# Adding the residual by accumulating stores: an early copy into the output, and four stores from GpSimd that add onto it

## The reference, cut to what matters

```python
    mix = jax.nn.sigmoid(gate_conv) * y_conv + jax.nn.sigmoid(gate_m) * y_m
    x = x + rmsnorm(jnp.einsum('btd,de->bte', mix, w_o), g_post_mix)

    hf = rmsnorm(x, g_pre_ff)
    ff = jnp.einsum('btf,fd->btd', jnp.square(jax.nn.relu(jnp.einsum('btd,df->btf', hf, w_ff1) + b_ff1)), w_ff2) + b_ff2
    x = x + rmsnorm(ff, g_post_ff)
```

## Time and profile before

| | |
|---|---|
| Median of 3 runs | 1226.94 us (1226.82 to 1227.23) |
| The profiled execution's own time | 1226.39 us |
| Its span | 1224.8 us |
| Mean granted TensorE clock | 0.996 of full speed |
| TensorE busy | 1200.2 us, 98% of the span |
| DVE, ACT, POOL busy | 866.0, 544.0, 65.4 us |

### The profile page before, as it was taken

The page is one execution under the profiler, slowest core; times in us unless marked ns, Lnnn a source line. Parts: engine busy times, 40 slices in busy tenths (PEclk is TensorE's granted clock), DMA queues, the critical chain, the costliest instruction groups (busy, mean ns, idle before and its releaser), DMA issues.

```text
span 1224.8 us, 22983 instructions
## 1 busy us (share of the span) xinstructions
PE 1200.2 (98%) x8893; PEld 1128.2 (92%) x8893; DVE 866.0 (71%) x1275; ACT 544.0 (44%) x836; POOL 65.4 (5%) x129
## 2 busy tenths in 40 slices
PE   9999999999999999999999999999999999999995
PEld 9999978989797898879999999999999999999994
DVE  6933788988888898887455434338687587585897
ACT  7533443453454345435543222246655453454543
POOL 4020001101100110110000000000000000000000
PEclk9999999999999999999999999999999999999998
DMA  6354226516432651623223232432433233333332
GB/s 222 104 160 147 70 71 222 199 34 224 170 130 69 222 199 34 239 105 104 87 86 88 85 97 74 158 105 67 145 104 104 87 87 104 87 93 98 86 125 73
DMA packets 44680, 145.95 MB, mean 119 GB/s; under 512 B 4756, under 2 KB 7188, under 8 KB 44232
## 3 DMA queue, kind: packets, MB, share of 16 engines
q1 hardware_dynamic: 33048, 103.74, 26.6%
q0 software_dynamic: 11424, 41.23, 9.6%
q10 hardware_dynamic: 144, 0.09, 0.0%
HBM read 120.54 MB, written 24.49 MB: 118 GB/s over the span
## 4 chain that ended last, share of the span: by engine, by line
PE 94%; DVE 3%; ACT 1%; issue 1%; DVEq 0%; POOL 0%; ACTq 0%; POOLq 0%
PE product L2051 73%; PE side L2051 21%; DVE yacc L2041 0%; PE side L2236 0%; ACT yacc L1294 0%; DVE yacc L1942 0%; ACT hhi L1159 0%; ACT cq L1139 0%; DVE hlo L1878 0%; DVE yacc L2045 0%; ACT whi L765 0%; DVE wlo L1916 0%; DVE wlo L1917 0%; DVE common L1942 0%; DVE wlo L1923 0%
## 5 line engine op out<-in xcount | busy, mean ns | idle before, releaser
L2051 PE MATMUL product<-ahi,whi 128*128 128x272 f32 x1232 | 261.7, 292 | 2.8 <-DVE cq L1860 1.6
L2051 PE MATMUL product<-ahi,wlo 128*128 128x272 f32 x1232 | 256.9, 288 | 0.0
L2051 PE MATMUL product<-alo,whi 128*128 128x272 f32 x1232 | 256.9, 288 | 0.0
L1322 DVE TENSOR_TENSOR wlo<-wraw,whi 128x1024 fp32r<-128x1024 f32 x122 | 148.8, 1224 | 114.5 <-ACT whi L765 102.6
L765 ACT ACTIVATE whi<-wraw 128x1024 fp32r<-128x1024 f32 x122 | 127.9, 1054 | 199.3 <-PE product L2051 121.7
L2051 PEld LDWEIGHTS product<-ahi,whi 128*128 128x128 f32 x1232 | 194.8, 188 | 13.1 <-issue 12.3
L2051 PEld LDWEIGHTS product<-alo,whi 128*128 128x128 f32 x1232 | 194.6, 189 | 0.0
L2051 PEld LDWEIGHTS product<-ahi,wlo 128*128 128x128 f32 x1232 | 193.7, 189 | 0.0
L1535 DVE SCALAR_TENSOR_TENSOR accp<-u,wdw,accp 128x512 f32<-128x512 f32 x240 | 163.7, 745 | 0.7 <-DVE accp L1535 0.7
L2051 PE MATMUL side<-hhi,whi 128*128 128x272 f32 x252 | 73.0, 290 | 3.6 <-DVE yacc L1942 1.4
L2051 PE MATMUL side<-hlo,whi 128*128 128x272 f32 x252 | 72.5, 288 | 0.0
(11 more groups left out here) (348 smaller groups left out, 2464.8 us busy)
## 6 DMA issues: line engine op xcount, KB each, us to landing
wraw<-in_wstream SPq DMA_DIRECT2D x176, 512.0 KB, 3.7
crg<-in_c_in POOLq DMA_DIRECT2D x32, 512.0 KB, 6.7
out_c_s<-crg POOLq DMA_DIRECT2D x32, 512.0 KB, 3.2
hb<-head_rows POOLq DMA_DIRECT2D x4, 580.0 KB, 5.3
x<-in_xT SPq DMA_DIRECT2D x4, 544.0 KB, 6.5
sgm<-in_xT SPq DMA_DIRECT2D x1, 2176.0 KB, 9.3
x_rows<-yc SPq DMA_DIRECT2D x1, 2176.0 KB, 10.1
x1b<-x_rows SPq DMA_DIRECT2D x1, 2176.0 KB, 9.5
```

Source lines behind the costliest of these rows:

```text
L1322: V.tensor_tensor(wlo[:, k % RING, :, :], wraw[:, k % 2, :, :], whi[:, k % RING, :, :].bitcast(f32), ALU.subtract).then_inc(lo_done, 1)
L2051: return pe.matmul(out, lhsT, rhs, start=start, stop=stop, skip_group_check=check)
```

## The change

The residual is copied into the output tensor `yT` itself, by the same early instruction that used to fill the scratch tensor. DVE only multiplies in the tail. GpSimd issues the four final stores, with `accum_op=ALU.add`: such a store adds its bytes to what lies at the destination. It waits for the early copy (`x1_moved`) and for each multiplication (`y_scaled`). The fetch of `x1b` is gone, and the scratch tensor too. The buffer of the first "down" unit's `s1` moves to a room of `yacc` that is still unused then, and its wait for an earlier product with it.

```diff
-        x1b = at("x1b", [P, KT, TT], f32, tmp0)
-        x1_dram = nc.dram_tensor("x1_rows", (P, KT, TT), f32, kind="Internal").ap()
+        first_s1 = at("first_s1", [P, KT // 2, P], f32, free_ + (KT - 2) * TT * 4)
+        def s1_of(d):
+            return s1[d % 2] if d > 0 else first_s1
...
             sp.wait_ge(x1_ready, 2 * KT)
-            sp.dma_start(x1_dram, yc[:, :, :]).then_inc(x1_moved, 16)
+            sp.dma_start(yT, yc[:, :, :]).then_inc(x1_moved, 16)
...
-            product_of(sp, WHEN["down", GROUPS - 2, IN_GROUP - 1], "P3")
-            sp.wait_ge(x1_moved, 16)
-            sp.dma_start(x1b[:, :, :], x1_dram).then_inc(x1_moved, 16)
-            for g in range(2):
-                part = slice(HALF * g, HALF * (g + 1))
-                for half in range(2):
-                    tiles = slice(KT // 2 * half, KT // 2 * (half + 1))
-                    sp.wait_ge(out_dve, 2 * g + half + 1)
-                    sp.dma_start(yT[:, tiles, part], yacc[:, tiles, part]).then_inc(out_saved, 16)
...
             pool.dma_start(n_p, npn[:, :, :]).then_inc(small_saved, 16)
+            pool.wait_ge(x1_moved, 16)
+            for g in range(2):
+                part = slice(HALF * g, HALF * (g + 1))
+                for half in range(2):
+                    tiles = slice(KT // 2 * half, KT // 2 * (half + 1))
+                    pool.wait_ge(y_scaled, 2 * g + half + 1)
+                    pool.dma_start(yT[:, tiles, part], yacc[:, tiles, part], accum_op=ALU.add).then_inc(out_saved, 16)
...
-                sum_1, n = s1[d % 2][:, :, :], SUMS * d
+                sum_1, n = s1_of(d)[:, :, :], SUMS * d
...
-                if d < 2:
+                if d == 1:
                     dve.wait_ge(chunk_done, C_FF + KT)
-                else:
+                if d > 1:
                     dve.wait_ge(split_lo, SPLIT_AT[DOWNS[d - 2], "sums"])
...
-            dve.wait_ge(x1_moved, 32)
             for g in range(2):
...
-                for half in range(2):
-                    tiles = slice(KT // 2 * half, KT // 2 * (half + 1))
-                    dve.wait_ge(y_scaled, 2 * g + half + 1)
-                    V.tensor_tensor(yacc[:, tiles, part], yacc[:, tiles, part], x1b[:, tiles, part], ALU.add).then_inc(out_dve, 1)
```

More of the change, by code:

```diff
@@ L437, in hybrid_layer @@
         tail_stat, tail_root = sem("tail_stat"), sem("tail_root")
-        y_scaled, out_dve = sem("y_scaled"), sem("out_dve")
+        y_scaled = sem("y_scaled")
         block = ctx.enter_context(nc.Block())
@@ L1175, in sums_split @@
                 act.activation(whi[:, 1, 0:KT // 2, :], s2[:, :, :], ACT.Copy)
-                act.activation(whi[:, 1, KT // 2:KT, :], s1[order_of(t) % 2][:, :, :], ACT.Copy).then_inc(split_hi, 1)
+                act.activation(whi[:, 1, KT // 2:KT, :], s1_of(order_of(t))[:, :, :], ACT.Copy).then_inc(split_hi, 1)
             def second_split(t):
@@ L1916, in sums_low @@
                 V.tensor_tensor(wlo[:, 1, 0:KT // 2, :], s2[:, :, :], whi[:, 1, 0:KT // 2, :].bitcast(f32), ALU.subtract)
-                V.tensor_tensor(wlo[:, 1, KT // 2:KT, :], s1[order_of(t) % 2][:, :, :], whi[:, 1, KT // 2:KT, :].bitcast(f32),
+                V.tensor_tensor(wlo[:, 1, KT // 2:KT, :], s1_of(order_of(t))[:, :, :], whi[:, 1, KT // 2:KT, :].bitcast(f32),
                                 ALU.subtract).then_inc(split_lo, 1)
```

## The result

The changed kernel takes 1235.97 us (median of 6 runs, 1235.33 to 1236.81) against 1226.88 us before (6 runs, 1226.59 to 1228.05): 9.1 us slower, ratio 1.0073 with a 95% interval of 1.0061 to 1.0086. The prediction was 1231.9 us in a range of 1223.0 to 1238.0, slower with a chance of 0.62. The profiled execution took 1235.73 us, with a span of 1234.2 against 1224.8.

The account below looks back on a forecast made before the run. TensorE bounds all up to the last matmul, then the tail; without DVE's additions the store queue sets the end. Half-rate stores and a held fourth move the last byte from 1223.85 to 1228.85: 1226.94 + 5.0 = 1231.9 us, range 1223.0 to 1238.0.

Parts of the forecast that it names:

- What is free: Early part and waits: copy into the output, removed x1b fetch, moved buffer and GpSimd's new waits cost or bring nothing.
- the most the change can bring: DVE's tail: without the four additions DVE ends 4.8 us earlier, the largest gain if stores cost what they do.
- Case P: Final stores: the adding is free, last byte at 1220.1, -3.7 us, time 1223.2 us; chance 0.18.
- Half the rate by a second read: Final stores: the old value is read too, so each store takes 3.08 us at 181 GB/s, not 1.54.
- in every row: Ground for the store rate: reads and writes of one transfer overlap in all profile rows.
- The hold: GpSimd's queue: 4 x 1024 descriptors don't fit, so the fourth store waits until the third has landed, plus 0.33 us.
- W: Final stores: two reads, half rate, fourth store held; last byte 1228.85, +5.0 us, time 1231.9 us; likeliest, chance 0.33.
- N: Final stores: two reads, half rate, no hold; last byte 1226.4, +2.55 us, time 1229.5 us; chance 0.22.
- first bytes move at 1212.62 + 0.02 + 0.90 + 0.55: First final store: half-multiplication's end, issue, preparation with two descriptors a run, then start of bytes: 1214.1.
- S: Final stores: worse than half rate, 121 GB/s, +8.7 us or with a hold +11.2, 1235.6 to 1238.1 us; chance 0.18.

Follow-up runs that it names:

- e10: Changed kernel with its four final stores plain and issued by SP, residual not added: 1222.97 us, ratio 0.9967 to the kernel before.
- e2: Changed kernel with its four GpSimd stores plain, so the residual is not added: 1225.08 us, ratio 0.9982 to the kernel before.
- e1: Changed kernel with GpSimd's descriptor room raised from 4096 to 5120 bytes: 1231.3 us, ratio 1.0036 to the kernel before.
- e3_early: Kernel before with the early copy going into the output tensor and the residual fetched back from there, tail as before: 1227.02 us, ratio 1.0003.
- e5_rows: Changed kernel with 5120 bytes of descriptor room and four accumulating stores of two whole tiles (128 runs of 4352 bytes): 1233.16 us, ratio 1.0047.
- e4_tile_less: Changed kernel whose fourth store carries three of its four tiles, old descriptor room: 1231.09 us, ratio 1.0036 to the kernel before.
- e11: Kernel before with the first quarter's addition computed by GpSimd and SP storing the second quarter first: 1228.47 us, ratio 1.0007.
- e6_one_quarter: Kernel before, early copy into the output, first quarter by GpSimd's accumulating store, each second-half addition behind its own multiplication: 1227.4 us, ratio 0.9997.

## Why the prediction was right, and where it was too small

The runs part the 9.1 us into four terms, each a difference of two of them, every kernel taken against the kernel before of its own session:

| | us | from |
|---|---|---|
| DVE's additions gone | -4.0 | e10 against before (-4.03) |
| Issued by GpSimd | +2.2 | e2 (-1.87) against e10 |
| Adding in the transfer | +6.2 | e1 (+4.35) against e2 |
| Fourth store held | +4.7 | after (+9.09) against e1 |

The intervals of the ratios leave each term open by 1.5 to 2 us. The traces give nearly the same terms with less scatter: from the first multiplication to the end of the span it is 13.47 us before, 9.54 in e10, 11.49 in e2, 17.52 in e1 and 22.02 after, so -3.9, +2.0, +6.0 and +4.5.

- **What is free** (the copy, the lost fetch, the moved buffer, the waits of GpSimd's empty queue): right; e3_early shows it for the copy and the scratch tensor. The lost fetch and the moved buffer are in e1, e2 and e10 and show no cost there; neither was tried alone.
- **The additions, "the most the change can bring"**: 4.8 us earlier on DVE was right. In the time it is 4.0, since the plain stores then queue for 6.2 us on the DMA engines. Case P had -3.7, but for stores from GpSimd, and for those e2_plain gives only -1.9: P too had GpSimd's start too early.
- **Half the rate by a second read**: right in kind and near in size. The steady rate is 195 to 200 GB/s, 0.54 to 0.55 of 362, where I took 0.50. That each byte is what costs, and not each run, is shown by e5_rows. That it is a second read is argued, not shown: it rests on two signs, the halved rate and the room that a store fills, near that of a load with twice the runs. No view shows the read itself, and an adding step that passes some 200 GB/s would look the same. My ground that reads and writes overlap "in every row" had no row either: none shows them apart. The Trainium skill's page "Collectives: The Full Stack", section "The bandwidth ceiling: the fold count and why AG ≠ RS ≠ AR", gives a ratio of 1.93 for its two collectives. Here it is 1.81 to 1.86 (362 against 200 and 195 GB/s).
- **The hold**: right in place, cause and pattern. The third store landed at 1226.9 and the fourth began at 1227.21, 0.3 us behind, against 0.33 in the earlier trace rows. The term was mis-sized: W stood 2.45 us over N, and measured it is 4.7. In the trace the gap without bytes is 3.0 us, and the lone fourth store, with a slow start of its own, takes 3.5 us where its bytes at the steady rate would take 2.8.
- **The sizes**, which took W from +5.0 to +9.1. The first step that fell short is "first bytes move at 1212.62 + 0.02 + 0.90 + 0.55", 2.8 us behind the start of the multiplications; measured, 4.0. The 0.02 was SP's; GpSimd needs 0.55 to 0.9 us from the release to the start of preparing a transfer. The trace of before has it, and my sum left it out: the store of the earlier trace rows issued at 542.20 was released by a DVE instruction that ended at 541.65. Preparation took 1.35 us, not 0.90. After that, in the profiled execution: the bytes of three stores 9.9 us for 9.2, because of the slow start; from there to the fourth's preparation 1.1 for 1.0; from that to its first bytes 1.9 for 1.45; its bytes 3.5 for 3.1; and 1.6 us in place of 0.95 behind the last byte. Together that is some 3.6 us on the 5.0, or 8.6 of the 9.1; what is left is within the scatter between executions.
- **The rivals**: P, that adding is free, falls with e2_plain against e1_ring. S, 121 GB/s, falls with the rate. By the time alone it would have looked right: 1235.97 lies in S's 1235.6 to 1238.1 and outside W's own 1230.9 to 1233. The whole range held the measured time only because S, whose mechanism was false, had widened it; that is luck, and what was right is the mechanism. N is what e1_ring is, and e4_tile_less but for one tile; they measured 1231.3 and 1231.1 where N gave 1229.5, short by the same late and slow start.

## What to carry to other kernels

An accumulating transfer takes the add off an engine and makes each byte cost the DMA engines about twice (195 to 206 GB/s against 362). Such a trade can pay only where those engines would be idle and nobody waits for the end, and no run here shows such a case; in a tail where the last store sets the time, four, two or one such store brought nothing or cost time. Before moving transfers to GpSimd's queue, read three things from the trace for that queue: how long from a release to the start of preparation, how long a preparation for so many runs, and after how many transfers in a row it stands still with no releaser. The last was a limit on descriptors here, and it made the fourth of four stores issued close together wait for the third to land.

## What the runs showed that was not expected

- GpSimd starts a DMA's preparation 0.55 to 0.9 us behind the instruction that releases it when it has been waiting long, SP 0.02 to 0.07 us. An ordinary instruction of GpSimd, the addition of e11, started 0.14 us behind its release, so by this one sample the lag is that of DMA issue.
- Preparing an accumulating store of 512 runs takes 1.27 to 1.93 us, a plain one 0.75 us; one of 1024 plain runs took 0.9. So a doubled count of descriptors, if it is one, is not all that makes it longer.
- The first accumulating bytes come slowly. One store alone, in e6_one_quarter, held the DMA engines for some 3.8 us, where its bytes at the steady rate would be 2.8.
- One GpSimd addition of 1088 elements a partition, 3.38 us long, held DVE's addition beside it, 3.45 us in place of 1.29.
